# Column transposes placed inside products, gate rows split over the entries, token sums told one by one

## The chip, the cores and the metric

The kernel runs on one core of a Trainium2 chip, as one program from launch to end. The metric is the device time in microseconds. TensorE (PE) multiplies 128x128 stationary blocks with up to 512 moving columns and writes PSUM, of which there are 8 banks of 128x512 fp32. VectorE (DVE), ScalarE (ACT) and GpSimd (POOL) work on SBUF, and DVE and ACT on PSUM too. SyncE (SP) issues the weight transfers. Each engine runs its own instruction stream in order, and the streams meet in semaphores.

## The reference

256 tokens of width 1024 go through two blocks, each two layers deep, all in fp32. The first block has four mixers side by side over one input projection:

```python
def first_block(x, ...):
    for l in range(DEPTH):                       # DEPTH = 2
        h = rms_norm(x, pre_norm_g[l])
        u = jnp.einsum('bsd,de->bse', h, w_in[l])
        u_mla, u_sb, u_moba, u_conv, u_gate = jnp.split(u, SPLITS, axis=-1)
        ...                                      # o_a, o_b, o_c, o_d: latent, stick-breaking,
                                                 # block-sparse attention, causal convolution
        y = jnp.concatenate([o_a, o_b, o_c, o_d], axis=-1) * jax.nn.silu(u_gate)
        y = jnp.einsum('bse,ed->bsd', y, w_out[l])
        x = x + rms_norm(y, post_norm_g[l])
    return x
```

The second block modulates, mixes, and runs a squared-ReLU network. Its mixer is a gated linear attention in layer 0 and a chunked attention with 16 heads in layer 1:

```python
def second_block(x, c, w_ada, b_ada, ln_g, ln_b, ...):
    c_act = jax.nn.silu(c)
    for i in range(DEPTH):                       # DEPTH = 2
        mods = jnp.split(c_act @ w_ada[i] + b_ada[i], 6, axis=-1)
        sh1, sc1, g1, sh2, sc2, g2 = [m[:, None, :] for m in mods]
        u = x * (1.0 + sc1) + sh1
        y = gla_mixer(u, ...) if i % 2 == 0 else chunk_attention(u, ...)
        x = layer_norm_2(DEEPNORM_ALPHA * x + (1.0 + g1) * y, ln_g[i, 0], ln_b[i, 0])
        u = x * (1.0 + sc2) + sh2
        y = squared_relu_mlp(u, ff_w1[i], ff_w2[i])          # square(relu(u @ w1)) @ w2
        x = layer_norm_2(DEEPNORM_ALPHA * x + (1.0 + g2) * y, ln_g[i, 1], ln_b[i, 1])
    return x
```

`g1` and `g2` are the gates that the change is about: each is a row of 1024 values, the same for all tokens.

## The kernel before

**Tiling.** The tokens are two tiles of 128 (`t` = 0, 1), `xt` and `xs` hold them as 128 tokens by 1024. For a projection they are needed the other way round: eight 128x128 transposes on PE turn a tile of `xs` (or `xt`) into two PSUM banks, and ACT (tile 0, and half of tile 1) and DVE (the other half of tile 1) copy them with scale and shift into `hT`, column block `k` = 0 to 7. Weights come in units of 1 MB into six slots `raw`, by transfers that SP issues in a fixed order as slots come free (`used`). `wait_landed` waits for a unit. PSUM is eight banks, `G[0..3]` and `A[0..3]`, given out by hand.

**Order.** Each engine's order is the order of its code; nothing is scheduled. PE's stream around the change is, for each stage `s` of the second block (0 mixer, 1 network, 2 attention, 3 network): transposes of tile 0, products of tile 0 (`unit_tile`, c = 0 and 1 of eight k each, with other products `beside` them), transposes of tile 1, products of tile 1. `stage_tile` waits for `xs` of its tile (`xn_ready`), `wait_tile` for each copied column.

**Seven products.** Larger products are done by a scheme with seven block products in place of eight. It needs sums of blocks: `token_sums` makes four sums of `hT` on DVE (`tsum`), `up_sums` and `weight_sums` those of the weights, `hidden_sums` those of the hidden values. `up_products` has three parts: "first tile", "half" and "rest". `out_product(l, half, j)` is one of seven products of an output projection, two 128x512 matmuls; `between` in the change goes between its two matmuls.

**Gate rows.** DVE builds the rows of `g1` and `g2` of a layer in `ada` (128 partial rows by 2048). `modulation` adds the partitions up by four matmuls with ones, each 512 values of a row, into the banks of `ROWB`; `gate_rows` adds bias and one into `gate_row`. The rows r = 0, 1 are `g1`, r = 2, 3 are `g2`. In the attention layer `ada` is later reused for sums of output weights.

**Boundaries.** Between the first block's layers `y_block`, `out_told` and `y_norm` on DVE and `y_square` and `x_square` on ACT normalize the projection's output and the new input; `layer_input` is ACT's copy into `hT`. Between network and attention `boundary` does it: `gated` multiplies by the gate, `residual` adds and takes the statistics, `normed` waits for ACT's root and writes `xs`.

Of the kernel before, what the change touches and what calls it, by code (L numbers as in the profile page):

```python
# [14 lines left out]
P = 128  # L15
S = 256
NT = S // P
D = 1024
# [117 lines left out]
def build(nc, x, units, cols, small, post_g, consts, onehot, rel_bias, ccol, crow_in, colb_in, ada_rows,  # L136
          ln_rows, low_in, gk_in, att_line, v_row, out):
    with ExitStack() as ctx:
# [15 lines left out]
        ROWB = ((G[2], G[3], A[3], A[0]), (A[1], A[2], A[3], A[0]))  # L154
# [225 lines left out]
        tsum_ready, usum_ready = event("tsum_ready", 1), event("usum_ready", SEVEN - 1)  # L380
# [58 lines left out]
        OUT_W.append([[ada[:, 0:D], ada[:, D:2 * D], row(tline), crow[:]],  # L439
# [161 lines left out]
        def _(act):  # L601
# [74 lines left out]
            for l in range(DEPTH):  # L676
# [233 lines left out]
        def _(dve):  # L910
# [223 lines left out]
            for l in range(DEPTH):  # L1134
# [188 lines left out]
            def gate_rows(lay):  # L1323

                dve.wait_ge(row_in, 16 * (lay + 1))
                for r, (g, h, b) in enumerate(zip((0, 0, 1, 1), (0, 1, 0, 1), ROWB[lay])):
                    dve.wait_ge(modr_psum.sem, modr_psum.at(lay, 1 + r // 3))
# [66 lines left out]
            def boundary(s, y_waits):  # L1394
# [58 lines left out]
            def mixer_block(m, k, told, a, b, op=ALU.add):  # L1453
# [4 lines left out]
                ch.do(dve.tensor_tensor(ytmp[:, t, c], a, b, op))  # L1458
                ch.sync()
# [67 lines left out]
            def token_sums(s, tsum, told):  # L1527
# [5 lines left out]
                ch.do(dve.tensor_tensor(tsum[:, 2], b[1][1], b[0][1], ALU.subtract))  # L1533
                ch.sync(1)
                ch.do(dve.tensor_tensor(tsum[:, 1], b[1][1], tsum[:, 0], ALU.subtract))
                ch.sync()
                dve.tensor_tensor(tsum[:, 3], b[1][0], tsum[:, 1], ALU.subtract).then_inc(told, 1)  # L1537
# [95 lines left out]
            def groups(s):  # L1633
# [3 lines left out]
                token_sums(s, tsum, tsum_ready.sem)  # L1637
                square(s)
                hidden_sums(s, 0, 0)
                for g in range(SEVEN - 1):  # L1640
# [65 lines left out]
            gate_rows(0)  # L1706
# [121 lines left out]
            def queries(qd):  # L1828
                dve.wait_ge(bc_ready.sem, bc_ready.at(qd, 1))
                if qd == 0:  # L1830
                    wait_used(dve, 0, N_ATT)
                    q = G[0][:]
# [6 lines left out]
            def value_rows(qd):  # L1839
# [3 lines left out]
                for t in range(NT):  # L1843
                    v = G[2][:, t * GW:(t + 1) * GW].rearrange("p (c n) -> p c n", c=2) if qd == 0 else csum[:, t:4:2]
# [55 lines left out]
            gate_rows(1)  # L1900
# [15 lines left out]
        def _(pe):  # L1916
# [75 lines left out]
            def out_product(l, half, j, free=None):  # L1992
# [13 lines left out]
                if half == 1:  # L2006
                    mm.then_inc(op_ready.sem, 1)
# [795 lines left out]
```

## Time and profile before

| | us |
|---|---|
| median of 3 runs | 1003.79 (1003.29 to 1005.03) |
| the profiled execution | 1003.1 |
| its span, first to last instruction | 1001.3 |
| PE busy | 979.4 |
| DVE busy | 789.4 |
| ACT busy | 206.9 |
| POOL busy | 82.6 |

The profile is of one execution. A line like `L2227` is a line of the kernel before. An fp32 matmul leaves two records in the trace, a transpose one. Records of PE overlap, since matmuls are pipelined: the distance between two starts is the cost of one, its own length is not. "Idle" in brackets is the time in which the engine had no record, with what ended it.

### The profile page before, as it was taken

The numbers are of one execution on the slowest core, as the hardware profiler recorded it, in microseconds if no ns is written. First come the engines' busy times: TensorE is split into PE (matmuls) and PEld (weight loads), VectorE is DVE, ScalarE is ACT, GpSimd is POOL, SyncE is SP. The second block draws the span as 40 slices with busy tenths as digits, with TensorE's granted clock in tenths as the row PEclk, the third lists the DMA queues.
The fourth block names the chain that finished last, engine by engine and source line by source line (L and its number), as shares of the span: only waits on it lengthen the run. The fifth ranks groups of instructions, "written<-read, shape, count | busy, mean of one in ns | idle before, by whom it ended". The sixth has DMA issues, their size and how long they took to land. (4 is left out here: it accounts for less than half of the span.)

```text
span 1001.3 us, 14199 instructions
## 1 busy us (share of the span) xinstructions
PE 979.4 (98%) x5306; PEld 718.2 (72%) x5306; DVE 789.4 (79%) x1785; ACT 206.9 (21%) x504; POOL 82.6 (8%) x91
## 2 busy tenths in 40 slices
PE   8999999999999999999999999999999999999996
PEld 5858764858866799757777777668995677777763
DVE  2697687596677889888999888965888877766677
ACT  4134324115232221102000000022223210000101
POOL 1100000000000000000002000026850000000020
PEclk9999999999999999999999999999999999999998
DMA  9955553856454766555779777524453354645511
GB/s 358 350 216 187 206 184 153 330 195 247 169 199 179 273 221 250 203 200 198 261 259 362 272 255 256 207 85 169 157 186 122 126 174 171 218 176 177 177 44 42
DMA packets 29916, 205.58 MB, mean 205 GB/s; under 512 B 3630, under 2 KB 3795, under 8 KB 6172
## 3 DMA queue, kind: packets, MB, share of 16 engines
q1 hardware_dynamic: 27116, 191.60, 52.6%
q0 software_dynamic: 2736, 13.11, 3.5%
q8 instruction: 42, 0.69, 0.3%
q14 instruction: 22, 0.18, 0.1%
HBM read 203.64 MB, written 1.05 MB: 204 GB/s over the span
## 5 line engine op out<-in xcount | busy, mean ns | idle before, releaser
L1923 PE MATMUL bank<-hT,raw 128*128 128x256 f32 x736 | 162.5, 380 | 0.0
L1923 PEld LDWEIGHTS bank<-hT,raw 128*128 128x128 f32 x736 | 138.7, 190 | 20.4 <-issue 1.7
L2251 PE MATMUL bank<-yT,arena 128*128 128x512 f32 x224 | 101.0, 594 | 0.6 <-DVE yT L1593 0.4
L2251 PE MATMUL bank<-raw,arena 128*128 128x512 f32 x180 | 86.9, 593 | 0.0
L2251 PEld LDWEIGHTS bank<-yT,arena 128*128 128x128 f32 x224 | 42.3, 190 | 55.1 <-issue 51.2
L953 DVE CUSTOM_DVE_ANT_0 raw<-raw,crow 128x1024 f32<-128x1024 f32 x64 | 75.4, 1220 | 1.4 <-DVEq L129 1.4
L2278 PEld LDWEIGHTS bank<-hT,raw 128*128 128x128 f32 x416 | 50.5, 192 | 12.4 <-issue 12.4
L800 ACT ACTIVATE arena<-bank 128x512 f32<-128x512 f32 x28 | 16.7, 597 | 195.9 <-PE bank L2278 195.9
L2278 PE MATMUL bank<-hT,raw 128*128 128x128 f32 x416 | 50.6, 275 | 0.0
L986 DVE SCALAR_TENSOR_TENSOR arena<-arena 128x256 f32<-128x256 f32 x120 | 48.4, 480 | 0.1
L1556 DVE TENSOR_TENSOR arena<-arena 128x256 f32<-128x256 f32 x28 | 13.5, 481 | 38.1 <-ACT arena L800 37.9
L2278 PE MATMUL bank<-arena,gateT 128*128 128x128 f32 x336 | 42.4, 276 | 0.9 <-DVE arena L1537 0.9
L940 DVE SCALAR_TENSOR_TENSOR ada<-raw,cact,ada 128x1024 f32<-128x1024 f32 x28 | 36.6, 1307 | 7.1 <-DMA raw<-units_dram 6.5
L2278 PE MATMUL bank<-arena 128*128 128x128 f32 x336 | 42.2, 275 | 0.0
L2251 PEld LDWEIGHTS bank<-raw,arena 128*128 128x128 f32 x180 | 29.9, 191 | 16.3 <-issue 16.3
L2227 PE MATMUL bank<-hT,raw 128*128 128x128 f32 x256 | 37.7, 283 | 3.7 <-ACT hT L668 3.6
L2278 PEld LDWEIGHTS bank<-arena,gateT 128*128 128x128 f32 x336 | 39.7, 192 | 1.3 <-DVE arena L1537 1.3
L2001 PE MATMUL bank<-arena 128*128 128x512 f32 x88 | 39.7, 592 | 0.0
L2278 PEld LDWEIGHTS bank<-arena 128*128 128x128 f32 x336 | 39.7, 192 | 0.0
L2278 PEld LDWEIGHTS bank<-arena,raw 128*128 128x128 f32 x224 | 29.4, 192 | 13.4 <-issue 13.4
L2227 PEld LDWEIGHTS bank<-hT,raw 128*128 128x128 f32 x256 | 33.0, 191 | 6.2 <-issue 5.2
L802 ACT ACTIVATE arena<-bank 128x384 f32<-128x384 f32 x28 | 13.8, 491 | 106.4 <-PE bank L2278 106.4
(462 smaller groups left out, 1814.6 us busy)
## 6 DMA issues: line engine op xcount, KB each, us to landing
raw<-units_dram SPq DMA_DIRECT2D x180, 1024.0 KB, 5.0
arena<-ln_rows_dram POOLq DMA_DIRECT2D x4, 1024.0 KB, 5.0
arena<-att_line_dram POOLq DMA_DIRECT2D x4, 512.0 KB, 6.1
arena<-small_dram POOLq DMA_DIRECT2D x2, 896.0 KB, 9.6
arena<-ada_rows_dram POOLq DMA_DIRECT2D x1, 1536.0 KB, 7.4
xt<-x_dram SPq DMA_DIRECT2D x2, 512.0 KB, 4.2
arena<-post_g_dram POOLq DMA_DIRECT2D x2, 512.0 KB, 8.8
kst<-consts_dram SPq DMA_DIRECT2D x1, 608.0 KB, 14.1
```

What stands on the lines that cost most here:

```text
L800: act.activation(prod[:, 0:4].rearrange("p i n -> p (i n)"), A[0][:], ACT.Copy).then_inc(prod_ready.sem, 1)
L802: act.activation(prod[:, 4:7].rearrange("p i n -> p (i n)"), A[0][:, 0:3 * P], ACT.Copy).then_inc(prod_ready.sem, 1)
L940: ins = dve.scalar_tensor_tensor(dst, w, cc, dst, ALU.mult, ALU.add)
L953: ins = dve.tensor_tensor_reduce(out=w, in0=w, in1=crow[:], scale=1.0, scalar=0.0, op0=ALU.mult, op1=ALU.add, accum_out=dst[:, c:c + 1])
L986: ins = dve.scalar_tensor_tensor(cacc[:, c, :], xg[:, c, j:j + S], w, cacc[:, c, :], ALU.mult, ALU.add)
L1556: ch.do(dve.tensor_tensor(csum[:, 0:5:4], prod[:, 0:1].to_broadcast([P, 2, P]), prod[:, 1:3], ALU.add))
L1923: mm = pe.matmul(b[:, c * S:(c + 1) * S], raw[:, s, k * 256 + c * P:k * 256 + (c + 1) * P], act_t[:, k, :], start=(k == 0), stop=(k == KC ...
L2001: mm = pe.matmul(OUT_BANKS[l][j][:], x[c] if isinstance(x, list) else x[:, c], y[c] if isinstance(y, list) else y[:, 512 * c:512 * (c + 1) ...
L2227: mm = pe.matmul(b[:, c * S + t * P:c * S + (t + 1) * P], raw[:, n % SLOTS, k * 256 + c * P:k * 256 + (c + 1) * P], hT[:, k, t * P:(t + 1) ...
L2251: mm = pe.matmul(SB[i][:], x, y, start=g == 0, stop=stop)
L2278: mm = pe.matmul(A[0][:, i * P:(i + 1) * P], x(k), y(k), start=k == 0, stop=k == 3)
```

## The change

It has six parts.

1. `out_product` may run something between its two matmuls. The transposes of tile 0 of the second block's input (`input_transposes(0)`) and of the first network's input (`stage_tile(1, 0)`) are put there, in the last product of the projection ahead of them. `input_transposes(1)` goes in front of the fourth gate-row product.
2. `unit_tile(..., held=2)` leaves the last two columns of c = 1 for `unit_rest`, which runs behind the transposes of tile 1 (networks and attention).
3. The four gate-row products of the second layer are split: row 0, transposes, row 1 at the attention's entry, rows 2 and 3 in the second network ahead of tile 1's transposes. DVE takes rows 2 and 3 up after `hidden_sums(3, 0, 0)`. Since `ada` is held longer, one sum of output weights goes to `xs`.
4. The first values of the attention are computed beside the columns of tile 0, not behind them.
5. `token_sums` tells each sum by itself, and "half" takes the product that needs the earliest first.
6. At the layer boundary the last block and its square go ahead of the column copies, and in `boundary` the second tile's `gated` goes behind the first tile's `normed`.

```diff
-        ROWB = ((G[2], G[3], A[3], A[0]), (A[1], A[2], A[3], A[0]))
+        ROWB = ((G[2], G[3], A[3], A[0]), (A[1], A[2], A[1], A[2]))
...
-        OUT_W.append([[ada[:, 0:D], ada[:, D:2 * D], row(tline), crow[:]],
+        OUT_W.append([[ada[:, 0:D], xs[:, 1, :], row(tline), crow[:]],
...
                     x_square(l + 1, 0)
                     y_square(l, 1, 0)
-                    layer_input(l + 1, 0, 0, 3)
                     y_square(l, 1, 1)
-                    layer_input(l + 1, 0, 3, KC)
+                    layer_input(l + 1, 0, 0, KC)
                     x_square(l + 1, 1)
...
                     x_scale(l + 1, 0)
+                out_told(l, 7, 3, s2, A[1][:], ALU.subtract)
                 y_block(l, 2)
-                out_told(l, 7, 3, s2, A[1][:], ALU.subtract)
                 y_block(l, 3)
...
                 residual(s, 0)
-                if s % 2:
-                    gated(s, 1, 0, y_waits[2])
                 normed(s, 0)
-                for h in range(s % 2, 2):
+                for h in range(2):
                     gated(s, 1, h, y_waits[2 + h])
...
+                else:
+                    dve.tensor_tensor(tsum[:, 2], b[1][1], b[0][1], ALU.subtract).then_inc(told, 1)
+                    ch.sync()
+                    dve.tensor_tensor(tsum[:, 1], b[1][1], tsum[:, 0], ALU.subtract).then_inc(told, 1)
+                    dve.wait_ge(told, parts + 2)
+                    dve.tensor_tensor(tsum[:, 3], b[1][0], tsum[:, 1], ALU.subtract).then_inc(told, 1)
...
                 hidden_sums(s, 0, 0)
+                if s == 3:
+                    gate_rows(1, (1,))
...
                     if c == 0 and free is not None:
                         mm.then_inc(used[free % SLOTS], 1)
+                    if c == 0 and between is not None:
+                        between()
...
-                    for k in range(KC):
+                    for k in range(KC - c * held):
...
+            def unit_rest(n, b, t, held):
+
+                for k in range(KC - held, KC):
+                    unit_columns(n, b, t, 1)(k)
...
                 elif part == "half":
+                    pe.wait_ge(usum_ready.sem, usum_ready.at(lay, g))
                     pe.wait_ge(tsum_ready.sem, tsum_ready.at(lay, 1))
-                    pe.wait_ge(usum_ready.sem, usum_ready.at(lay, g))
-                    product(2, lambda k: u[:, 1, k], lambda k: tsum[:, 1, k])
-                    product(3, lambda k: u[:, 2, k], lambda k: tsum[:, 2, k]).then_inc(up_half.sem, 1)
+                    product(3, lambda k: u[:, 2, k], lambda k: tsum[:, 2, k])
+                    pe.wait_ge(tsum_ready.sem, tsum_ready.at(lay, 2))
+                    product(2, lambda k: u[:, 1, k], lambda k: tsum[:, 1, k]).then_inc(up_half.sem, 1)
...
-                    start=k % 4 == 0, stop=k % 4 == 3))
+                    start=k % 4 == 0, stop=k % 4 == 3), held=2)
+                if s == 3:
+
+                    pe.wait_ge(ob_ready.sem, ob_ready.at(HEADS, 3))
+                    modulation(1, 2, 4)
+
                 stage_tile(s, 1)
+                unit_rest(up[0], A[3], 0, 2)
                 unit_tile(s, up[0], A[3], 1)
...
-                    modulation(0)
+                    modulation(0, 0, 3)
+                    input_transposes(1)
+                    modulation(0, 3, 4)
...
-            out_product(MIXER, 1, 3)
-
+            out_product(MIXER, 1, 3, between=lambda: stage_tile(1, 0))
             net(1)
 
-            modulation(1)
...
+            modulation(1, 0, 1)
+            stage_tile(2, 0)
+            modulation(1, 1, 2)
...
-            stage_tile(2, 0)
-            unit_tile(2, N_ATT, G[0], 0, after=3)
-            value_tile(0, 0)
+            wait_landed(pe, 0, N_ATT + 2)
+            unit_tile(2, N_ATT, A[3], 0, value_column(0), held=2)
             stage_tile(2, 1)
-            unit_tile(2, N_ATT, G[0], 1)
+            unit_rest(N_ATT, A[3], 0, 2)
+            unit_tile(2, N_ATT, A[3], 1)
             unit_t(0, N_ATT + 1, hT, G[1])
-            value_tile(0, 1)
-            pe.wait_ge(gate_used.sem, 4)
+            for k in range(KC):
+                mm = value_column(1)(k)
+            mm.then_inc(used[(N_ATT + 2) % SLOTS], 1)
+            pe.wait_ge(gate_used.sem, 3)
```

On ACT, at the boundary between the first block's two layers (`hT` is the transposed input, `ssy` the sum of squares of an output block, `root` a square root; the difference in one piece):

```order
 L637 ACTIVATE arena,ssy<-gateT 128x512
 L640 ACTIVATE ybias<-ssy,eps_x 128x1
-L653 ACTIVATE hT<-bank,pre 128x128 x3
-L637 ACTIVATE arena,ssy<-gateT 128x512
-L643 ACTIVATE root<-ssy,ybias 128x1
-L653 ACTIVATE hT<-bank,pre 128x128 x5
+L637 ACTIVATE arena,ssy<-gateT 128x512
+L643 ACTIVATE root<-ssy,ybias 128x1
+L653 ACTIVATE hT<-bank,pre 128x128 x8
```

The second square and the root, which stood behind three of the eight column copies, stand ahead of all eight.

On PE, where the second block's input enters, before the change (`arena,yT` are the last products of the projection, `kst` holds the identity, so that `kst,xt` are transposes; `hT,raw` are products of the first unit):

```order
L2001 MATMUL bank<-arena,yT 128x512 x4
L2203 MATMUL bank<-kst,xt 128x128 x8
L2227 MATMUL bank<-hT,raw 128x128
L2239 MATMUL bank<-hT,raw 128x128
L2227 MATMUL bank<-hT,raw 128x128
```

and after it:

```order
L2008 MATMUL bank<-arena,yT 128x512 x3
L2023 MATMUL bank<-kst,xt 128x128 x8
L2008 MATMUL bank<-arena,yT 128x512
L2246 MATMUL bank<-hT,raw 128x128
L2263 MATMUL bank<-hT,raw 128x128
L2246 MATMUL bank<-hT,raw 128x128
```

One 128x512 product has moved from in front of the transposes to behind them.

On PE, where the attention layer's input enters, before the change (`ada,kst` are gate-row products, `kst,xs` transposes, `hT,raw` the columns of the first unit, `raw,hT` the values):

```order
L2318 MATMUL bank<-raw,arena 128x512 x8
L2194 MATMUL bank<-ada,kst 128x512 x4
L2203 MATMUL bank<-kst,xs 128x128 x8
L2227 MATMUL bank<-hT,raw 128x128 x16
L2520 MATMUL bank<-raw,hT 128x256 x8
L2203 MATMUL bank<-kst,xs 128x128 x8
L2227 MATMUL bank<-hT,raw 128x128 x16
```

and after it, from the first gate row to the third of the eight columns:

```order
L2220 MATMUL bank<-ada,kst 128x512
L2023 MATMUL bank<-kst,xs 128x128 x8
L2220 MATMUL bank<-ada,kst 128x512
L2246 MATMUL bank<-hT,raw 128x128
L2556 MATMUL bank<-raw,hT 128x256
L2246 MATMUL bank<-hT,raw 128x128
L2556 MATMUL bank<-raw,hT 128x256
L2246 MATMUL bank<-hT,raw 128x128
```

Two of four gate-row products have left, one stands behind the transposes, and each column of the first unit is followed by its column of the values.

## Rows read from the trace of the kernel before

**Rows 1.** The page's first part: busy time, share and instructions by engine.

```profile
PE 979.4 (98%) x5306; PEld 718.2 (72%) x5306; DVE 789.4 (79%) x1785; ACT 206.9 (21%) x504; POOL 82.6 (8%) x91
```

**Rows 2.** Waits of PE over the run: total us, times, longest us.

```profile
PE bank L2227 <- ACT hT L668: 3.6, 8, 1.3
...
PE bank L2203 <- DVE xs L1391: 1.8, 3, 1.5
...
PE bank L2278 <- DVE arena L1537: 0.9, 2, 0.5
```

**Rows 3.** Two windows: length, then PE, PEld, DVE, ACT, POOL busy, PEclk.

```profile
690.00:780.00 90.00, 90.00 (x683) 73.26 (x682) 74.99 (x209) 24.43 (x79) 42.02 (x38) 1.00 0.44 156
...
812.00:960.00 148.00, 148.00 (x849) 107.83 (x848) 105.06 (x222) 13.06 (x24) 0.54 (x1) 1.00 0.51 179
```

**Rows 4.** Timeline at the layer boundary (start, length, engine, line, tiles, count, [idle]).

```profile
162.97 0.68 DVE L1127 TENSOR_TENSOR gateT<-arena,bank 128x512 f32<-128x512 f32 x1
...
163.20 0.89 ACT L653 ACTIVATE hT<-bank,pre 128x128 f32<-128x128 f32 x3 [1.41 <-PE bank L1973]
...
163.97 0.64 ACT L637 ACTIVATE arena<-gateT 128x512 f32<-128x512 f32 x1
...
164.73 0.29 ACT L643 ACTIVATE root<-ssy,ybias 128x1 f32<-128x1 f32 x1
...
170.39 1.09 PE L1973 MATMUL bank<-kst,xs 128*128 128x128 f32 x8 [1.70 <-DVE xs L1066]
```

**Rows 5.** Timeline where the second block's first tile enters.

```profile
312.97 3.60 PE L2001 MATMUL bank<-arena,yT 128*128 128x512 f32 x8
...
316.41 1.03 PE L2203 MATMUL bank<-kst,xt 128*128 128x128 f32 x8
...
317.11 2.90 ACT L668 ACTIVATE hT<-bank,arena 128x128 f32<-128x128 f32 x8 [5.53 <-PE bank L2203]
...
317.82 0.46 PE L2227 MATMUL bank<-hT,raw 128*128 128x128 f32 x2 [0.38 <-ACT hT L668]
```

**Rows 6.** Timeline at the second tile of the first network.

```profile
458.85 0.81 DVE L1391 TENSOR_SCALAR xs<-xt,bag,rst 128x1024 f32<-128x1024 f32 x1
...
459.71 1.10 PE L2203 MATMUL bank<-kst,xs 128*128 128x128 f32 x8 [0.15 <-DVE xs L1391]
...
464.79 0.69 DVE L1535 TENSOR_TENSOR arena<-hT,arena 128x512 f32<-128x512 f32 x1
...
466.25 2.05 PE L2278 MATMUL bank<-arena,gateT 128*128 128x128 f32 x16 [0.45 <-DVE arena L1537]
```

**Rows 7.** Timeline where the attention layer's first tile enters.

```profile
656.67 3.60 PE L2194 MATMUL bank<-ada,kst 128*128 128x512 f32 x8
...
656.99 0.68 DVE L1357 TENSOR_TENSOR arena<-bank,arena 128x512 f32<-128x512 f32 x1
...
658.34 0.81 DVE L1391 TENSOR_SCALAR xs<-xt,bag,rst 128x1024 f32<-128x1024 f32 x1
...
660.11 1.04 PE L2203 MATMUL bank<-kst,xs 128*128 128x128 f32 x8
...
662.41 3.81 PE L2227 MATMUL bank<-hT,raw 128*128 128x128 f32 x32 [1.27 <-ACT hT L668]
...
666.06 3.62 PE L2520 MATMUL bank<-raw,hT 128*128 128x256 f32 x16
```

**Rows 8.** Timeline at the second tile of the second network.

```profile
794.88 1.09 PE L2203 MATMUL bank<-kst,xs 128*128 128x128 f32 x8 [1.49 <-DVE xs L1391]
...
801.42 2.05 PE L2278 MATMUL bank<-arena,gateT 128*128 128x128 f32 x16 [0.45 <-DVE arena L1537]
...
804.14 0.43 DVE L1556 TENSOR_TENSOR arena<-arena 128x256 f32<-128x256 f32 x1 [0.76 <-ACT arena L800]
...
806.85 0.69 DVE L1593 TENSOR_TENSOR yT<-yT,raw 128x512 f32<-128x512 f32 x1
...
808.56 3.60 PE L2251 MATMUL bank<-yT,arena 128*128 128x512 f32 x8
```

More of the change, by code:

```diff
@@ L1989, in first_units, with out_product @@
                         mm.then_inc(used[u % SLOTS], 1)
-            def out_product(l, half, j, free=None):
+            def out_product(l, half, j, free=None, between=None):
                 u, d, w = OUT_UNITS[l][2 * half:2 * half + 2], OUT_D[l][half], OUT_W[l][half]
@@ L2005, in out_product, with transposes, input_transposes @@
                         mm.then_inc(used[free % SLOTS], 1)
+                    if c == 0 and between is not None:
+                        between()
                 if half == 1:
                     mm.then_inc(op_ready.sem, 1)
+            def transposes(s, t, src, banks):
+                for q in range(2):
+                    for i in range(4):
+                        c = 4 * q + i
+                        mm = pe.transpose(banks[q][:, i * P:(i + 1) * P], src[:, t, c * P:(c + 1) * P], ident)
+                    mm.then_inc(tp_ready.sem, 1)
+            def input_transposes(t):
+                pe.wait_ge(x_new.sem, x_new.at(DEPTH, t + 1))
+                transposes(0, t, xt, UB[t])
             pe.wait_ge(zeros_ready, 1)
@@ L2186, in _, with modulation @@
                 out_product(l, 0, 3)
-                out_product(l, 1, 3)
-            def modulation(lay):
+                if l < DEPTH - 1:
+                    out_product(l, 1, 3)
+                else:
+                    out_product(l, 1, 3, between=lambda: input_transposes(0))
+            def modulation(lay, r0, r1):
                 wait_used(pe, 0, (U1 + A_AT[3], ADA_1[23])[lay])
-                for b, c in zip(ROWB[lay], (0, 512, D, D + 512)):
-                    mm = pe.matmul(b[:], ones, ada[:, c:c + 512], start=True, stop=True)
-                    if b is A[3] or b is A[0]:
+                for r in range(r0, r1):
+                    mm = pe.matmul(ROWB[lay][r][:], ones, ada[:, 512 * r:512 * (r + 1)], start=True, stop=True)
+                    if r % 2:
                         mm.then_inc(modr_psum.sem, 1)
-            def transposes(s, t, src, banks):
-                for q in range(2):
-                    for i in range(4):
-                        c = 4 * q + i
-                        mm = pe.transpose(banks[q][:, i * P:(i + 1) * P], src[:, t, c * P:(c + 1) * P], ident)
-                    mm.then_inc(tp_ready.sem, 1)
             def stage_tile(s, t):
@@ L2216, in wait_tile, with unit_tile @@
                     pe.wait_ge(us_dve.sem, us_dve.at(s, k - 3))
-            def unit_tile(s, n, b, t, beside=None, after=0):
+            def unit_tile(s, n, b, t, beside=None, after=0, held=0):
                 wait_landed(pe, 0, n)
@@ L2344, in net @@
                     up_products(s, n, g + 1, "rest")
+                    if s == 3 and g == 0:
+                        pe.wait_ge(gate_used.sem, 4)
                     seven_products(s, down[g], g, 1)
@@ L2378, in _ @@
             for t in range(NT):
-                pe.wait_ge(x_new.sem, x_new.at(DEPTH, t + 1))
-                transposes(0, t, xt, UB[t])
                 n = N_GLA + GW_AT[1]
```

52 lines of the change are left out of this document (26 added, 26 removed).

## The prediction, made before the changed kernel was run

> **What bounds the kernel now.** I read four views in this order. The page's first part says that PE is busy for 979.4 of 1001.3 us and that no other engine comes near [rows 1]. So a change can only pay if it removes work from PE or fills its idle time, and all idle time together is 22 us, a part of it after the last matmul, in the closing normalization, which the diff does not touch. Second, PE's waits name what ended the rest: copies of transposed columns into hT by ACT (3.6 us in 8 waits), the normalized rows xs by DVE (1.8 us in 3 waits here, and the layer boundary of rows 4), and the token sums (0.9 us in 2 waits) [rows 2]. Third, the windows show that the long middles of the attention layer and of the second network are without a gap: 90.00 of 90.00 us and 148.00 of 148.00 us busy, with the granted clock at 1.00 [rows 3]. Fourth, the timelines at the stage entries, where all of the named waits lie [rows 4 to 8]. There I went from each PE start back to the instruction that it waited for.
>
> Two spacings serve throughout. One fp32 128x512 product leaves two records; eight records take 316.41 - 312.97 = 3.44 us, so one product costs 0.86 us [rows 5]. Thirty-two 128x128 records take 666.06 - 662.41 = 3.65 us, of which 0.07 is start-up after a wait, so one 128x128 product costs 0.224 us and a set of eight transposes (eight records) 0.90 us [rows 7].
>
> **The layer boundary.** The change puts the square of the last output block ahead of the column copies on ACT, and on DVE it makes that block one 512-wide instruction (0.60 us) earlier. Now the block is made at 162.97 and its square starts only at 163.97, behind three copies; the root starts at 164.73 and the transposes of tile 1 at 170.39, after 1.70 us of idle PE [rows 4]. After the change the block ends near 163.05, the square starts there, and the root some 0.9 us earlier. DVE, however, has the same three 0.7 us instructions to do (the block is the middle one today) and is through with them at 162.97 + 2 x 0.70 = 164.4; today it goes on at 164.73 + 0.29 = 165.05. So the chain gains 0.6 us, not 0.9. The price is that eight copies of 0.30 us (0.89/3) now start at 164.1 instead of 163.2, which delays PE's first tile by 0.75 us; it is hidden in the 1.70 us of idle time, of which about 0.5 is left. Bounds: 0 (if the late copies were the new end) and 0.9. I take 0.6.
>
> **The second block's two input tiles.** The transposes of tile 0 move in front of the last product of the output projection, those of tile 1 in front of the fourth gate-row product. Today PE waits after the transposes, 317.82 against 317.3, and starts up slowly: the first pair of records takes 0.46 us, which is 0.07 more than later ones [rows 5]. Moved 0.86 us ahead, the transposes start at 315.55, ACT's first copy at 316.25 (0.70 behind, as now) and the first column is there at 316.95, while PE has work until 317.3. Both the wait and the start-up go: 0.6 us, and again 0.6 at tile 1, whose rows are the same. The last block of the projection comes 0.9 us later, but ACT reads it only after its 2.90 us of copies, which themselves start 0.86 earlier. A return from transposes to an open accumulation is not in the trace without a wait; the switch the other way costs nothing at 316.41 [rows 5]. Bounds for both places together: 0 (the wait returns at the switch back) and 1.2. I take 1.2, nearest to that row.
>
> At these places the idle rows and the spacing disagree: the idle column shows 0.38 us, the starts show 0.6, because the first records after a wait cannot hide behind a predecessor. The Trainium skill has this in "TensorE: Matmul & The Clock Gate", section "Part 2: What happens when you issue a matmul": the drain of one matmul overlaps the fill of the next, and an isolated one can't hide it. By that rule the spacing is right and the sum is the 5.3 us below; by the idle column it would be the 3.9 us of the first rival. The slow first pair behind the wait agrees with the rule [rows 5].
>
> **The first network.** Its tile 0 transposes also move one product ahead, which fills 0.6 us. That is not worth anything: the next thing is tile 1, whose xs is ready at 458.85 + 0.81 = 459.66, and PE is idle in front of it already [rows 6]. The DVE chain to that xs hangs on earlier products, so it stays where it is, and PE only waits longer. The two held-back products (0.45 us) fill the wait for tile 1's first copy, but the end of tile 1 is set by DVE's last column copies, so this is hidden too. What counts is the token sums. All four are told at once today, and PE goes on at 466.25, after 0.45 us idle plus a slow start [rows 6]. The second product in the new order needs only the sum of 464.79 + 0.69 = 465.48, before PE gets there (466.25 - 0.6). Bounds 0.45 (the idle row) and 0.7 (the spacing); I take 0.65.
>
> **Entry to the attention layer.** Today: four gate-row products from 656.67 (3.43 us), transposes at 660.11, a wait of 1.4 us for ACT's fourth column until 662.41, tile 0, and eight value products [rows 7], then a second wait of 0.4 us of the same kind, so 2.3 us without issue. After: one gate row, until 657.53. Tile 0's normalization is no longer behind the 0.68 us instruction at 656.99, so that its xs is finished 0.3 us earlier than 658.34 + 0.81, at 658.85, and the transposes start there: a new wait of 1.3 us. Then the second gate row (until 660.65) covers the first copies, and the value columns, 0.43 us each beside 0.224 us, make a step of 0.655 us per column against 0.36 us per copy, so that no copy is waited for. Tile 1's xs is ready near 664.7, its transposes are reached only at 667.2, and the two held products cover most of its first copy; 0.3 us of pacing stays. Without issue 1.6 us, so 0.7 us gained. Bounds: -0.6 (xs not earlier and the interleaving of two stationary operands costs 0.04 us a time) and 1.3 (xs in time).
>
> **Rows three and four of the second layer's gate.** Two products of 0.86 us, 1.7 us in all, leave the busy entry above and go to the second network, in front of tile 1's transposes. There PE is idle for 1.49 us until 794.88 [rows 8], and the two held products add 0.45: 1.94 us of room for 1.7 us. The held products afterwards cover the wait for the first copy. So 1.7 us go; bounds 1.2 (if bank or row waits push them 0.5 us late) and 1.7.
>
> **The token sums there** give the same 0.7 us at 801.42, but DVE now adds two gate-row additions of some 0.62 us before the sums for group 1. It had 0.76 us of idle time before 804.14 [rows 8]; PE brings that instruction's input 0.7 earlier, yet DVE gets to it 0.5 later, and the last weight sum, now 807.54, comes at 808.05. PE asks for it at 808.56 - 0.70 = 807.86, so 0.25 us are lost again. Bounds -0.1 and 0.7; I take 0.45.
>
> **The sum.** 0.6 + 1.2 + 0.65 + 0.7 + 1.7 + 0.45 = 5.3 us. All lower ends together would be 0.95, all upper ends 6.2. The profiled execution took 1003.1 us (span 1001.3), so 997.8; the median of the runs shown is 0.7 above it, so 998.5. Once for all: less than 0.2%, 2 us, a measurement of this kernel can't tell from no change.
>
> **Rivals.**
> First, only what the idle column shows is given back, since switching costs what start-up cost: 0.6 + 0.75 + 0.45 + 0.2 + 1.7 + 0.2 = 3.9 us, 999.9. For it speaks that no row shows the switch back; against it the spacing at 316.41.
> Second, the new waits bite where I count them as hidden: both gains by token sums go to DVE (1.1 us) and the boundary is held by the late copies (0.6): 1000.2. For it speaks that DVE is 105 of 148 us busy and comes only a few tenths ahead of PE in each group; against it its idle 0.76 us there.
> Third, the change doesn't do what it says at the switches and entries, and only the moved rows count: 1003.8 - 1.7 = 1002.1.
> Fourth, slower: TensorE's clock. The new wait of 1.3 us before the attention tile and the longer one of about 1.2 us in the first network could let the clock fall to 1.2 GHz. A tile unit of 3.6 us then takes 3.6 us more; from 5.3 us of work at the lower level on, the change loses, and with three such units the time is 998.5 + 10.8 = 1009. Against it: waits of 1.70 and 1.49 us stand in this trace [rows 4, 8] and the transposes right behind them take 1.09 us, against 1.04 behind work without a gap [rows 7]; at half the clock they would take twice as long.
>
> **How the numbers follow.** Forecast 0.70 (own range 997.3 to 999.5), first rival 0.13, second 0.08, third 0.05, slower 0.03, and 0.01 for the rest. Faster by over 0.2% needs less than 1001.8: forecast, first and second rival, less a share for a chance offset of the runs, 0.89. The third and that share make no change 0.07, slower 0.04. The range goes from 996.8 (upper ends, less half a us between runs) to 1001.2, past the second rival.
>
> **What will show it.** In the waits of PE the entry "<- ACT hT" falls from 3.6 us to about 1, and "<- DVE arena" from 0.9 to under 0.4. The tile transposes before the second block stand 0.86 us ahead of a last 128x512 product, with no idle at the first column. The wait for tile 1's xs at the boundary is about 0.5 us. The entry to the attention layer has one wait, for xs, near 1.3 us. In the second network the gate-row products lie in front of transposes that still wait a few tenths. PE busy falls by little, since nothing is removed, and the idle sum falls by 4 to 5 us. Wrong would be: a wait on DMA, idle time in the attention window, or a clock below 1.00 before the last matmul.

## The result, and the profile after

The changed kernel takes 998.21 us (median of 6 runs, 997.62 to 999.45), the one before 1004.41 us (6 runs, 1003.29 to 1005.63) on the same chip. The ratio is 0.994, interval 0.993 to 0.9951: faster by about 6 us.

The profiled execution took 999.45 us, its span is 997.7. First the page's first part, as in [rows 1].

```profile
PE 977.9 (98%) x5306; PEld 718.3 (72%) x5306; DVE 788.7 (79%) x1785; ACT 206.6 (21%) x504; POOL 81.6 (8%) x91
```

The same 5306 PE instructions, 1.5 us less busy. The fences from here on show only the rows that the text speaks of; rows that stand between them in time are left out. Then the waits of PE (total, times, longest), against [rows 2].

```profile
PE bank L2023 <- DVE xs L1390: 2.8, 4, 1.2
PE bank L1980 <- DVE xs L1064: 2.8, 3, 2.0
PE bank L1992 <- ACT hT L653: 2.1, 2, 1.1
PE bank L1972 <- POOL zeros L485: 1.3, 1, 1.3
PE bank L2275 <- DVE yT L1598: 0.4, 1, 0.4
PE bank L2246 <- ACT hT L668: 0.4, 1, 0.4
```

The waits of the second block's tiles for ACT's column copies fell from 3.6 us in 8 to 0.4 us in one, and the token sums' 0.9 us is gone from the list. Waiting for xs grew from 1.8 to 2.8 us. The two windows without a gap of [rows 3] are still that:

```profile
690.00:780.00 90.00, 90.00 (x663) 71.69 (x662) 76.81 (x211) 24.41 (x79) 41.81 (x38) 1.00 0.47 165
812.00:960.00 148.00, 148.00 (x845) 107.35 (x844) 104.27 (x221) 13.66 (x25) 4.01 (x3) 1.00 0.50 173
```

Now the stage entries, PE and what it waits for. The layer boundary, the answer to [rows 4]; this whole profile lies 2.05 us late here, for a reason that comes below, so distances are to be compared, not times.

```profile
164.42 0.68 DVE L1125 TENSOR_TENSOR gateT<-arena,bank 128x512 f32<-128x512 f32 x1
164.56 1.09 PE L1980 MATMUL bank<-kst,xs 128*128 128x128 f32 x8 [0.51 <-DVE xs L1064]
165.13 0.64 ACT L637 ACTIVATE arena<-gateT 128x512 f32<-128x512 f32 x1 [1.29 <-DVE gateT L1125]
166.09 2.16 ACT L653 ACTIVATE hT<-bank,pre 128x128 f32<-128x128 f32 x8
166.59 4.97 PE L1992 MATMUL bank<-raw,hT 128*128 128x352 f32 x16 [0.94 <-ACT hT L653]
171.80 0.44 PE L1980 MATMUL bank<-kst,xs 128*128 128x128 f32 x2 [0.24 <-DVE xs L1064]
```

The square follows its block at once, all eight copies stand behind it, and from tile 0's transposes to tile 1's it is 171.80 - 164.56 = 7.24 us; before, 170.39 - 162.51 = 7.88. The second block's first tile, the answer to [rows 5]:

```profile
316.96 1.04 PE L2023 MATMUL bank<-kst,xt 128*128 128x128 f32 x8
317.83 1.02 PE L2008 MATMUL bank<-arena,yT 128*128 128x512 f32 x2
318.69 0.38 PE L2246 MATMUL bank<-hT,raw 128*128 128x128 f32 x2
```

The transposes stand in front of the last product, and nothing waits: 0.87 and 0.86 us from start to start, and the first pair of records takes 0.38 us, not 0.46. The second tile of the first network, against [rows 6]:

```profile
459.90 1.09 PE L2023 MATMUL bank<-kst,xs 128*128 128x128 f32 x8 [1.21 <-DVE xs L1390]
460.83 0.61 PE L2263 MATMUL bank<-hT,raw 128*128 128x128 f32 x4
461.28 4.71 PE L2246 MATMUL bank<-hT,raw 128*128 128x128 f32 x32
465.82 1.95 PE L2302 MATMUL bank<-arena,gateT 128*128 128x128 f32 x16
```

The wait for xs is 1.21 us instead of 0.15, the wait for the token sums is none. But thirty-two records take 465.82 - 461.28 = 4.54 us where work without waits needs 3.58: short waits for columns lie inside that group. The attention's entry, against [rows 7]:

```profile
655.98 1.02 PE L2220 MATMUL bank<-ada,kst 128*128 128x512 f32 x2
658.17 1.09 PE L2023 MATMUL bank<-kst,xs 128*128 128x128 f32 x8 [1.18 <-DVE xs L1390]
659.10 1.02 PE L2220 MATMUL bank<-ada,kst 128*128 128x512 f32 x2
659.96 0.38 PE L2246 MATMUL bank<-hT,raw 128*128 128x128 f32 x2
660.18 0.60 PE L2556 MATMUL bank<-raw,hT 128*128 128x256 f32 x2
```

One gate row, the wait for xs, transposes, the next gate row, then columns and values in turn. And the second network, against [rows 8]:

```profile
789.72 1.88 PE L2220 MATMUL bank<-ada,kst 128*128 128x512 f32 x4
791.82 1.09 PE L2023 MATMUL bank<-kst,xs 128*128 128x128 f32 x8 [0.22 <-DVE xs L1390]
...
803.92 1.02 PE L2275 MATMUL bank<-raw,arena 128*128 128x512 f32 x2
804.88 3.70 PE L2275 MATMUL bank<-yT,arena 128*128 128x512 f32 x8
```

Rows three and four fill the wait for xs: 0.22 us left of 1.49.

**Where the span went.** It is only 3.6 us shorter (997.7 against 1001.3), because the first 128x256 product starts at 23.78 us and not at 21.72. The same kernel was run again to see whether the changed program always starts 2 us later or this was a chance of one execution, as was expected: its second profile has that product at 21.70 and a span of 995.5, and its six times have a median of 997.76 us (997.33 to 999.89). Behind that product 973.88 and 973.85 us remain in the two profiles, 979.60 before. So the change is worth 5.7 us, and the late start is not part of it. What happened there the windows show (length, PE, PEld, DVE, ACT, POOL, PEclk, DMA share, GB/s); here the changed kernel's first profile:

```profile
6.00:8.00 2.00, 0.27 (x2) 0.00 (x0) 1.34 (x5) 0.70 (x4) 0.00 (x0) 1.00 0.92 349
...
12.00:14.00 2.00, 2.00 (x5) 1.20 (x4) 0.00 (x0) 0.00 (x0) 0.00 (x0) 0.50 1.01 380
14.00:16.00 2.00, 2.00 (x8) 1.28 (x7) 0.00 (x0) 0.00 (x0) 0.00 (x0) 0.94 1.02 422
```

PE had 0.27 us of work in 2 us, and then the granted clock fell to 0.50, which is the 1.2 GHz level. This is the wait of 2.0 us for xs (L1064) in the list above; 1.1 us of waiting for hT follow. In the second profile the longest such wait is 0.8 us, the window 6 to 8 us has 1.82 us of PE work, and the clock stays at 1.00. But a long wait alone is not the whole cause. Three variants of the next section have waits of 2.01, 2.25 and 2.38 us in the same place (`copies_ahead`, `none_held`, `sums_told_at_once`), and their clock stays at 1.00 through the start. The first of them has nearly the schedule of the profile above:

```profile
8.39 1.06 PE L1987 MATMUL bank<-kst,xs 128*128 128x128 f32 x8 [2.01 <-DVE xs L1064]
```

```profile
12.00:14.00 2.00, 1.84 (x7) 0.94 (x6) 0.00 (x0) 0.00 (x0) 0.00 (x0) 1.00 1.03 405
```

From the first 128x352 product to tile 1's transposes it takes 15.71 - 10.45 = 5.26 us there, 17.00 - 10.47 = 6.53 us at the lower clock, and 14.93 - 9.87 = 5.06 us in the kernel before. So of the 2.06 us by which the first profile is late, 1.47 lie in the stretch with the lower clock and 0.60 in front of it. What decides whether the clock falls behind such a wait, no run here shows.

**Stage by stage**, in distances between starts of PE instructions (changed kernel, second profile). "Input" is from the last eight records of the projection to the products of the chunk states. "Entry" runs from the first gate row to the first 128x256 product. "Half" is from tile 1's transposes to the first of the products that use a token sum (the first half product), and "seven" is from there to the product behind it. In the last row the third number runs from that product to the one that uses the last weight sum.

| us | before | changed | gain | forecast |
|---|---|---|---|---|
| boundary, tile 0 to tile 1 | 7.88 | 7.25 | 0.63 | 0.6 |
| input | 82.67 | 81.45 | 1.22 | 1.2 |
| network 1, half and seven | 6.54 + 1.89 | 5.92 + 1.79 | 0.72 | 0.65 |
| entry | 18.10 | 15.83 | 2.27, of which 1.72 moved | 0.7 + 1.7 |
| network 2, tile 0 to tile 1 | 8.55 | 8.55 | 0 in spite of 1.72 added | 0 |
| network 2, half and seven, less the late weight sum | 6.53 + 1.89 + 5.26 | 5.92 + 1.79 + 5.36 | 0.61 | 0.45 |

The rows make 5.45 us of gain. The rest to 5.75 is in long stretches between them that the change doesn't touch: the first network's middle took 188.53 us before and 188.33 here (188.28 to 188.47 in the variants below), the attention layer behind its entry 111.56 and 111.46.

### The profile page after: what moved, and what is told of

Its sections match the earlier page's. It is cut to its first block and busy times, and to the rows that moved or that the text cites. A ratio compares the mean times of both kernels' runs of the same rounds, so it can differ in the third digit from the quotient of the medians.

```text
span 997.7 us, 14231 instructions
## 1 busy us (share of the span) xinstructions
PE 977.9 (98%) x5306; PEld 718.3 (72%) x5306; DVE 788.7 (79%) x1785; ACT 206.6 (21%) x504; POOL 81.6 (8%) x91
```

## The experiments

All start from the changed kernel and are judged by these distances, which repeat to about 0.02 us in stages that an edit leaves alone. The first two concern the boundary: which of its two orders matters? DVE's order left as before, ACT's as changed:

```diff
-                out_told(l, 7, 3, s2, A[1][:], ALU.subtract)
                 y_block(l, 2)
+                out_told(l, 7, 3, s2, A[1][:], ALU.subtract)
                 y_block(l, 3)
```

> The changed kernel, at the layer boundary with ACT's new order but VectorE's old one (last output block one instruction later). Measured from the first transposes of tile 0 to those of tile 1: 7.88 us before, 7.24 us changed. Theory: the square starts as soon as the block is there, 0.6 us later than in the changed kernel, and VectorE waits for the root again: 7.55 us. Rival (ACT's order is the whole gain): 7.24. Rival (both are needed): 7.88.

And ACT's order as before, DVE's as changed:

```diff
                     y_square(l, 1, 0)
+                    layer_input(l + 1, 0, 0, 3)
                     y_square(l, 1, 1)
-                    layer_input(l + 1, 0, 0, KC)
+                    layer_input(l + 1, 0, 3, KC)
```

> The changed kernel, at the layer boundary with VectorE's new order but ACT's old one (three copies ahead of the square). Theory: the square starts behind the copies as before, so the distance from tile 0's to tile 1's transposes is 7.88 us again and VectorE's order alone is worth nothing. Rival: the parts add up, 7.55 us.

Measured: 7.59 us with ACT's order alone, 7.88 with DVE's alone, 7.25 with both. ACT's order brings 0.29, DVE's nothing by itself and 0.34 on top: an earlier block is of no use while its square stands behind three copies.

The run with ACT's order alone took 1001.41 us (one execution), more than the boundary explains. Its second network is 3.07 us longer, in a place that it shares with the changed kernel. Waits and timeline there:

```profile
955.30 5.10 POOL L598 TENSOR_TENSOR raw<-raw,arena 128x1024 f32<-128x1024 f32 x2 [95.40 <-DMA raw<-units_dram]
955.33 2.87 DVE L1555 TENSOR_TENSOR arena<-raw,arena 128x512 f32<-128x512 f32 x1
958.25 2.12 PE L2302 MATMUL bank<-arena 128*128 128x128 f32 x10 [1.85 <-DVE arena L1555]
```

POOL began an addition 0.03 us ahead of DVE's, and DVE's took 2.87 us instead of 0.69: it ended 0.35 us behind POOL's first of two, if each took half of the 5.10 us. PE stood for 1.85 us, and in the window behind it the clock fell:

```profile
956.00:960.00 4.00, 2.15 (x14) 1.96 (x13) 2.19 (x1) 0.00 (x0) 4.00 (x2) 0.84 0.00 0
960.00:964.00 4.00, 4.00 (x17) 2.85 (x17) 1.62 (x4) 0.60 (x1) 0.41 (x1) 0.74 0.01 4
```

In the changed kernel (second profile) the two additions begin at 954.33 and 954.32, DVE first, and DVE needs its 0.69. The next addition of DVE falls into POOL's second one; it takes 1.98 us for 0.42 and has slack; the kernel before has the same (1.97 us):

```profile
954.32 0.69 DVE L1555 TENSOR_TENSOR arena<-raw,arena 128x512 f32<-128x512 f32 x1
954.33 5.21 POOL L598 TENSOR_TENSOR raw<-raw,arena 128x1024 f32<-128x1024 f32 x2 [95.44 <-DMA raw<-units_dram]
...
957.85 1.98 DVE L1561 TENSOR_TENSOR arena<-arena 128x256 f32<-128x256 f32 x1 [2.83 <-ACT arena L798]
```

The Trainium skill states this rule in "SBUF — State Buffer", section "SBUF: two separate sides": VectorE with two SBUF inputs and a GpSimd operation that reads SBUF exclude one another, and whichever starts first keeps the port pair to its end. The rows agree where POOL is first. Where DVE is first it keeps its 0.69 us, but POOL's two additions take 5.21 us against 5.10, so that the rows don't show POOL held up for as long as DVE ran. That the pair of ports is the reason is read from these rows and the page; no run took POOL's addition out of the way. Nor do the runs show what decides which is first: the two profiles of the changed kernel have DVE ahead by 0.08 and by 0.01 us.

**The first network's transposes inside the product.** The forecast gave this no value.

```diff
-            out_product(MIXER, 1, 3, between=lambda: stage_tile(1, 0))
+            out_product(MIXER, 1, 3)
+            stage_tile(1, 0)
```

> The changed kernel with the first network's tile 0 transposes behind the last projection product again. Theory: nothing. From the first of the last eight projection records to tile 1's transposes it takes 10.59 us in both, because xs of tile 1 sets them; the wait in front of them shrinks from 1.21 to 0.6 us and a wait of 0.38 us for the first copy comes back. Rival (a filled gap pays): 0.6 us more, like at the input.

Measured: from the last records of the projection to tile 1's transposes 10.61 us against 10.59. Worth nothing, as forecast; tile 1's xs sets that time. This run (1001.05 us, one execution) met the same collision of POOL and DVE, a PE wait of 1.87 us for L1555 with the same fall of the clock behind it (0.83 and 0.74), and its second network is 3.1 us longer.

**The second block's input tiles.**

```diff
-                if l < DEPTH - 1:
-                    out_product(l, 1, 3)
-                else:
-                    out_product(l, 1, 3, between=lambda: input_transposes(0))
+                out_product(l, 1, 3)
+                if l == DEPTH - 1:
+                    input_transposes(0)
...
-                    modulation(0, 0, 3)
+                    modulation(0, 0, 4)
                     input_transposes(1)
-                    modulation(0, 3, 4)
```

> The changed kernel with both sets of input transposes of the second block put back behind the products (the last projection product, the fourth gate row). Theory: each place waits again 0.4 us for ACT's first copy and starts up slowly, 0.6 us each; from the first record of the last projection products to the first of the chunk-state transposes (81.45 us in the changed kernel) it takes 82.65 us, and the whole 1.2 us more. Rival (only the idle column counts): 0.75 us more. Rival (the mixer's own chain is the end there): 0.

Measured: input 82.71 us against 81.45, so 1.26 for two waits whose idle rows show 0.38 each. Timed 999.40 us, ratio 0.9952 (0.9934 to 0.997); the changed kernel in the same batch 997.76, ratio 0.9937 (0.9919 to 0.9955), the one before 1003.93.

**Token sums told at once.**

```diff
-                token_sums(s, tsum, tsum_ready.sem, tsum_ready.at(lay, 0))
+                token_sums(s, tsum, tsum_ready.sem)
...
-        tsum_ready, usum_ready = event("tsum_ready", 3), event("usum_ready", SEVEN - 1)
+        tsum_ready, usum_ready = event("tsum_ready", 1), event("usum_ready", SEVEN - 1)
...
-                    pe.wait_ge(tsum_ready.sem, tsum_ready.at(lay, 2))
...
-                    pe.wait_ge(tsum_ready.sem, tsum_ready.at(lay, 3))
```

> The changed kernel with the four token sums told at once again, the order of the two half products as changed. Theory: PE waits again for the last sum in both networks, 0.7 us in the first and 0.6 us in the second (where 0.1 us of a later stall goes away), 1.3 us in all. Rival (VectorE's chain is the end in the networks): the wait of 0.45 us comes back at both places, but the time grows by less than 0.3 us.

Measured: half and seven 6.62 + 1.86 us in both networks against 5.92 + 1.79, so 0.77 each; in the second 0.20 comes back further on, which leaves 0.57. The start-up is part of it: 0.07 to 0.1 us in the step behind the wait. Timed 999.35 us, ratio 0.9951 (0.9934 to 0.9968).

**Rows three and four behind tile 1's transposes.** If they only fill a wait, moving them behind it must cost.

```diff
-                if s == 3:
-                    pe.wait_ge(ob_ready.sem, ob_ready.at(HEADS, 3))
-                    modulation(1, 2, 4)
                 stage_tile(s, 1)
                 unit_rest(up[0], A[3], 0, 2)
+                if s == 3:
+                    pe.wait_ge(ob_ready.sem, ob_ready.at(HEADS, 3))
+                    modulation(1, 2, 4)
```

> The changed kernel with gate rows 2 and 3 of the second layer behind the second network's tile 1 transposes and held products, not in front. Theory: the transposes stay where they are, since xs sets them; of the 1.72 us of products 1.0 us is taken up by the pacing of tile 1 (its end is set by VectorE's copies), so the two half products start 0.7 us later and the rest of the kernel 0.6 us. Rival (every product outside the wait costs its length): 1.7 us later. Rival (all of it fits): 0.

Measured: half 8.35 us against 5.92, 2.43 more, and 1000.27 us (one execution); neither theory had that much. PE's rows:

```profile
790.20 1.09 PE L2023 MATMUL bank<-kst,xs 128*128 128x128 f32 x8 [1.93 <-DVE xs L1390]
791.13 0.92 PE L2263 MATMUL bank<-hT,raw 128*128 128x128 f32 x4
791.85 3.29 PE L2220 MATMUL bank<-ada,kst 128*128 128x512 f32 x4
794.98 3.73 PE L2246 MATMUL bank<-hT,raw 128*128 128x128 f32 x32
```

The transposes have nothing in front of them again, so PE waits 1.93 us, which is the room of 1.94 us that the forecast had worked out; then two gate-row products take 794.98 - 791.85 = 3.13 us instead of 1.72, and the held columns 0.72 instead of 0.45. The window has the reason:

```profile
788.00:792.00 4.00, 2.07 (x16) 1.88 (x15) 3.65 (x10) 1.34 (x5) 0.00 (x0) 0.91 0.00 0
792.00:796.00 4.00, 4.00 (x15) 2.21 (x14) 3.86 (x9) 0.46 (x2) 0.00 (x0) 0.66 0.00 0
```

The clock fell from 1.00 to a mean of 0.66. It cost 1.41 + 0.27 = 1.68 us; without it 2.43 - 1.68 = 0.75 would remain, near the 0.7 of the theory. That is an estimate: no run has this order at the full clock. The transposes right behind the wait took 1.09 us, as they do behind the other waits. The clock fell only after they had started, so their length does not tell whether a wait brings it down.

**No column held back, and two orders at the attention's entry.** Three kernels, one edit each: `held=0` for `held=2` (and 0 for 2 in `unit_rest`), tile 1's first gated half ahead of tile 0's normalization as before, and both gate rows ahead of tile 0's transposes.

```diff
-            unit_rest(N_ATT, A[3], 0, 2)
+            unit_rest(N_ATT, A[3], 0, 0)
```

```diff
+                if s % 2:
+                    gated(s, 1, 0, y_waits[2])
                 normed(s, 0)
-                for h in range(2):
+                for h in range(s % 2, 2):
```

```diff
-            modulation(1, 0, 1)
+            modulation(1, 0, 2)
             stage_tile(2, 0)
-            modulation(1, 1, 2)
```

> The changed kernel with no products held back behind tile 1's transposes, in either network or the attention layer. Theory: 0 in the first network (VectorE's copies end tile 1), 0.45 us in the attention layer (first gate row to the first 128x256 product: 15.82 us changed, 16.27 here), 0 to 0.1 in the second network: 0.5 us in all. Rival (held products cover a wait everywhere): 0.45 us at each of three places, 1.35 us.

> The changed kernel with the old order at the boundary into the attention layer: one gated multiplication of tile 1 ahead of tile 0's normalization. Theory: xs of tile 0 is 0.33 us later, and since PE waits for it, from the first gate row to the first 128x256 product it takes 16.15 us in place of 15.82. Rival (the wait is not the end there): no difference.

> The changed kernel with gate rows 0 and 1 both ahead of tile 0's transposes in the attention layer. Theory: the second row fills 0.86 us of the 1.18 us wait for xs, the transposes stay, and the wait for the first copy (0.45 us with start-up) comes back in place of 0.86 us of work: from the first gate row to the first 128x256 product 15.56 us in place of 15.82, a gain of 0.26 us. Rival (a row is worth most as a cover behind the transposes): 0.2 us slower.

Measured: the entry takes 16.27, 16.16 and 15.58 us, the changed kernel 15.83. Held columns bring 0.44 at the entry and nothing in the first network; in the second, 8.62 + 5.86 against 8.55 + 5.92 is no difference. The order of DVE brings 0.33. The split of rows one and two loses 0.25: the wait for xs is longer than a gate row, and the columns have the values beside them anyway. No run took the values from beside the columns alone; that they hide the copies is read from the rows of the entry, which show no wait there.

**Copies ahead of the up-sums.** Inside the 4.54 us group at 461.28 PE goes at the pace of the columns, and DVE comes late to its part of them:

```profile
459.76 0.68 DVE L1550 TENSOR_TENSOR gateT<-raw 128x512 f32<-128x512 f32 x1
460.36 0.68 DVE L1551 TENSOR_TENSOR gateT<-raw 128x512 f32<-128x512 f32 x1
460.97 0.68 DVE L1553 TENSOR_TENSOR gateT<-gateT,raw 128x512 f32<-128x512 f32 x1
461.68 0.69 DVE L1555 TENSOR_TENSOR gateT<-raw,gateT 128x512 f32<-128x512 f32 x1
462.29 1.36 DVE L1348 TENSOR_SCALAR hT<-bank,arena 128x128 f32<-128x128 f32 x4
```

Those are rows of the changed kernel: four additions for a weight that is used behind the copies. The edit makes two of them ahead of `stage_tiles`, which holds the copies, and two behind it, in both networks. It also takes the squares (L1522) ahead of the last token sum, and in the second network's group 0 the weight sums ahead of the half sums:

```diff
-            up_sums(UP[1][1], 1)
+            up_sums(UP[1][1], 1, 0)
             stage_tiles(3)
+            up_sums(UP[1][1], 1, 1)
...
+                    if s == 3 and g == 0:
+                        weight_sums(down[g])
+                        up_half_sums(s, g + 1)
```

> The changed kernel, on VectorE in both networks: tile 1's column copies between the first two and the last two weight sums, the square ahead of the fourth token sum, and in the second network group 0's weight sums ahead of the half sums. Theory: tile 1 is no longer paced by late copies; from tile 1's transposes to the first half product 5.92 us in the changed kernel, 5.45 here, in both networks, and in the second the stall of 0.1 us before the weight sums' product goes: 1.0 us in all. Rival (the late weight sums become the new wait of the half products): 5.9 us as before, or slower by some tenths.

Measured: half 5.31 us in both networks, 0.61 less. But the second network's long rest is 170.05 us instead of 169.64. PE waits there 0.25 us for the up-sum L1559, and its start comes 0.41 late. Timed 997.93 us (996.64 to 1001.19), ratio 0.9941 (0.9925 to 0.9957), no better than the changed kernel by this measure; behind its start 972.97 us, 0.88 less.

**All together.** On top of the edits of the run before, in that group the up-sums now go ahead of the hidden sums, and both gate rows ahead of the transposes; the new piece is:

```diff
+                    if s == 3 and g == 0:
+                        up_sums(up[g + 2], g + 2)
                     hidden_sums(s, g + 1, (g + 1) % 3)
```

> On top of the changed kernel: VectorE makes the first half of the up-sums before the copies of the input tiles and the second half behind them (as in the run with the copies ahead); both gate rows stand ahead of tile 0's transposes of the second network (as in the run with two rows ahead); and new, in group 0 of the second network's last pass, the up-sums of group 2 stand ahead of the hidden sums of group 1, because with the copies ahead TensorE waited there 0.25 us for the last up-sum and its products' starts came 0.41 us late. Theory (the 0.41 us was that one queue order on VectorE): the attention entry takes 15.58 us (the changed kernel 15.82), tile 1's transposes to the first half product 5.31 us in both networks (5.92), and the last product that uses a weight sum stands as far from the last hidden product as in the changed kernel (169.6, copies ahead 170.05); the span less its start is 972.4 us (changed 973.85). Rival (VectorE's load there is the bound, whatever the order): another wait comes in its place, the distance stays near 170.0 and the span less start near 972.8. Against the kernel before, timed: ratio 0.992 by the theory, with the changed kernel at 0.9937 to 0.994.

Measured: entry 15.58, half 5.32 and 5.32, rest 169.53, and behind its start 972.35 us. PE's rows in that place have no wait left:

```profile
806.22 1.95 PE L2313 MATMUL bank<-hT,raw 128*128 128x128 f32 x16
808.00 1.95 PE L2313 MATMUL bank<-arena 128*128 128x128 f32 x16
809.79 1.88 PE L2286 MATMUL bank<-raw,arena 128*128 128x512 f32 x4
```

So it was the order on DVE, and not DVE's load, that cost 0.41. Timed 996.43 us (996.12 to 997.27), before 1003.84: ratio 0.9921 (0.9906 to 0.9936). That is the fastest version of this study. Its distance to the changed kernel is 1.50 us in the traces; the intervals of the two ratios overlap, so the times alone don't show it.

## Why the prediction was right

The forecast was 998.5 us, the time 998.21, with 5.3 us of gain forecast and 5.7 found behind the start. Each term has the mechanism that the runs show, but that the time is met to 0.3 us is partly luck: the entry gave 0.15 us less and the second network's sums 0.16 more, 0.3 came from long stretches that the forecast gave nothing, and the median of the kernel before is 0.6 us higher over six runs (1004.41) than over the three that the forecast started from. One sum is wrong as written: all upper ends together make 0.9 + 1.2 + 0.7 + 1.3 + 1.7 + 0.7 = 6.5 us, not 6.2. The low end of the range, 996.8, does follow from 6.5. Point by point:

- *Boundary.* The chain gained 0.63 as said, and both of its halves were needed. About 0.5 us of idle was to be left before tile 1; it is 0.24. The first product is 0.82 us later than before behind the transposes (2.03 against 1.21), where 0.75 was expected, and that is hidden, though by little.
- *Input tiles.* 1.2 forecast, 1.22 found, 1.26 lost again when undone. The first rival, which took the idle column for the price, would have 0.75. It falls.
- *First network.* The moved set and the held columns are worth nothing, the token sums 0.72. Right.
- *Attention's entry.* Xs came early enough, the wait is 1.18 us (1.3 forecast), and columns with values run at 660.62 - 659.96 = 0.66 us a step, as worked out (0.655). Gained 0.55 and not 0.7: counted in spacings, the wait for xs costs 658.17 - 656.84 = 1.33, and 0.36 us of pacing stays in tile 1. The 2.3 us that the forecast took off for the kernel before is right, though the waits it names make 1.4 + 0.4 = 1.8; the rest is pacing of tile 1 there, 674.77 - 670.81 = 3.96 us for 3.58 of work. Unforeseen was that the second gate row is on the wrong side of the transposes.
- *Rows three and four.* 1.72 us, all hidden. Nothing pushed them late.
- *Second network's sums.* The late weight sum was mis-sized: PE loses 0.10 us there (804.88 against 804.78), not 0.25. So 0.61 and not 0.45. The second rival falls with it and with the boundary.
- *Clock.* The slower rival didn't happen in the changed kernel at the places it named: the clock there stays at 1.00 behind waits of 1.21 and 1.18 us. Its mechanism is real, though. Three variants, with waits of 1.93, 1.85 and 1.87 us, and one start show a fall. Where it can be worked out it cost less than I put on it, about 1.7 us in the second network and 1.5 in the start, not 3.6 a time. The argument against it was weak on both sides. It rested on two waits that left the clock at 1.00, of 1.70 and 1.49 us; the first of these lies close to the ones that did not, while waits of up to 2.38 us left it at 1.00 too. And it took transposes of 1.09 us for a sign of the full clock, which the run with a fall right behind such transposes refutes.
- *A sign of being wrong that did show.* "A clock below 1.00 before the last matmul" stands among them, and the first profile has it, 0.50 at 12 to 14 us. It lies in a stretch that the change does not touch, is absent from the second profile, and is not a failure of the forecast's mechanism; the sign was put too widely. The other two, a wait on DMA and idle time in the attention window, did not appear in that profile.

Not settled: why the wait for the first xs differs between executions (2.0 and 0.8 us), and why the clock fell behind one such wait and not behind three others of 2.01 to 2.38 us. The transfers run at 0.92 and 0.95 of their engines at 6 to 8 us there, and no run changed their order.

## What to carry to other kernels

A wait of TensorE costs its start-to-start spacing, 0.6 us here for 0.38 in the idle column, so short independent work put in front of the waiting instruction earns more than the waits list says. Before moving such work, look at what the next tile waits for: where the normalization of tile 1 sets the time, filling the wait of tile 0 is worth nothing, and where work stands in front of a wait it is free while behind it it is paid in full. Once PE's waits are down to tenths, the next gain is in the order of the engine that feeds it, and each reordering there has to be followed one group further.

## What the runs showed of the hardware

- A VectorE addition of 0.69 us takes 2.87 us when a GpSimd addition begins 0.03 us ahead of it, and keeps its 0.69 us when VectorE is first. In the other profiles VectorE leads by only 0.01 to 0.13 us, and two of the thirteen profiles of changed kernels had GpSimd first, at a price of 3.1 us, the fall of the clock included.
- The granted clock fell from 1.00 behind single waits of 1.93 us (mean 0.66 in 4 us), 1.85 us (0.84 and 0.74) and 1.87 us (0.83 and 0.74), and not behind one of 1.70 us. In the kernel's start it fell behind one of 2.00 us, but not behind 2.01, 2.25 and 2.38 us in other profiles. The length of a single wait does not decide it. It was back at 1.00 within 10 us each time, and had cost 1.7 us beside the 1.93 us of the wait.
- Distances inside a stage repeat to 0.02 us from profile to profile, while the start of the kernel varies from 21.68 to 23.78 us. For effects of some tenths, distances between two instructions decide where the whole time cannot.
